# Layer 0 of a two-layer trunk: index queries earlier, query scaling from level 1 of the search, one choice of keys ahead of attention instead of two, and level 6 of the recurrence's differences on ScalarE

## What is computed

```python
h = rms_norm(x, norm_mix_g[0])
z = h @ even_w_in[0]
aq, ak, av, iq, ik, iw, bq, bf, bi, bg = split_cols(z, EVEN_SPLITS)
aq = apply_rope(rms_norm(aq), cos, sin);  ak = apply_rope(rms_norm(ak), cos, sin)
iq = apply_rope(iq, cos_i, sin_i);        ik = apply_rope(ik, cos_i, sin_i)
# dsa_attention, for each block of 128 queries: an index score of all keys,
sc = einsum('bqhd,bsd->bqhs', iqb, ik)
score = einsum('bqhs,bqh->bqs', relu(sc) * IDX_DIM ** -0.5, iwb * IDX_HEADS ** -0.5)
_, sel = top_k(where(causal, score, -inf), 256)     # the 256 keys that a query may see
# ... then softmax attention of 8 heads (2 key heads) over the keys in sel
# hgrn2: a gated recurrence of 4 heads, in chunks; bt is the running sum of log f
att = einsum('bhtd,bhsd,bhtsd->bhts', qt, kt, exp(bt[:, :, :, None] - bt[:, :, None]))   # t >= s
o = att @ vt + (qt * exp(bt)) @ state
state = exp(b_last) * state + (kt * exp(b_last - bt)).T @ vt
x = x + concat(o_a, o_b) @ even_w_out[0];  x = x + square(relu(rms_norm(x) @ w_up)) @ w_down
```

## Time and profile before

| what | value |
|---|---|
| median of 3 runs | 2616.02 us (2614.91 to 2616.26) |
| profiled execution | 2613.89 us |
| its span in the trace | 2612.2 us |
| TensorE's mean granted clock | 0.969 |
| busy: PE, DVE, ACT, POOL | 2473.1, 1617.1, 1046.7, 1295.2 us |
| chain that ended last | PE 80%, DVE 11%, issue 4%, ACT 3%, POOL 2% |

### The profile page before, as it was taken

How to read it: one execution, slowest core, us unless ns; L and a number is a source line. 1 busy time by engine, 2 the same in 40 slices (tenths; PEclk the granted TensorE clock), 3 DMA queues, 4 the chain that set the end, 5 groups by cost and what they waited for, 6 DMA issues and landing times.

```text
span 2612.2 us, 31005 instructions
## 1 busy us (share of the span) xinstructions
PE 2473.1 (95%) x11111; PEld 1967.7 (75%) x11133; DVE 1617.1 (62%) x2334; ACT 1046.7 (40%) x1759; POOL 1295.2 (50%) x682
## 2 busy tenths in 40 slices
PE   6889797899989999999999999989999999999999
PEld 5677676455887788888888887757678888888887
DVE  6578779867995545644456756675355444654483
ACT  4255786556554323322222246444453222232220
POOL 4101233768873456654567621154516546664490
PEclk8999899899999999999999999979899999999999
DMA  4211123001300112111221231121201112211121
GB/s 146 60 30 29 41 61 93 17 13 30 108 9 17 51 62 64 56 40 32 64 64 32 73 109 41 33 83 32 52 33 53 36 40 64 64 42 39 48 64 65
DMA packets 164088, 136.67 MB, mean 52 GB/s; under 512 B 22985, under 2 KB 137746, under 8 KB 163986
## 3 DMA queue, kind: packets, MB, share of 16 engines
q1 hardware_dynamic: 152978, 125.10, 15.8%
q10 hardware_dynamic: 11008, 10.23, 1.5%
HBM read 116.17 MB, written 13.63 MB: 50 GB/s over the span
## 4 chain that ended last, share of the span: by engine, by line
PE 80%; DVE 11%; issue 4%; ACT 3%; POOL 2%; DMA 0%; ACTq 0%; DVEq 0%; POOLq 0%
PE ps L2342 23%; PE ps L2344 23%; PE ps L2343 23%; PE ps L2574 1%; PE ps L2562 1%; PE ps L2754 1%; PE ps L2582 1%; PE ps L2335 1%; PE ps L2476 1%; ACT signs L1337 1%; DVE ub L2229 1%; DVE ps L1887 1%; PE ps L2573 1%; DVE shared L2226 1%; DVE acc L2173 1%
## 5 line engine op out<-in xcount | busy, mean ns | idle before, releaser
L2342 PE MATMUL ps<-h_hi,w_hi 128*128 128x512 f32 x1680 | 669.3, 398 | 9.6 <-DVE h_lo L1639 4.3
L2343 PE MATMUL ps<-h_lo,w_hi 128*128 128x512 f32 x1680 | 658.4, 392 | 0.0
L2344 PE MATMUL ps<-h_hi,w_lo 128*128 128x512 f32 x1680 | 658.1, 392 | 0.0
L781 POOL TENSOR_TENSOR w_lo<-w_raw,w_hi 128x1024 fp32r<-128x1024 f32 x73 | 194.3, 2662 | 371.8 <-ACT w_hi L1347 366.7
L2342 PEld LDWEIGHTS ps<-h_hi,w_hi 128*128 128x128 f32 x1680 | 318.5, 190 | 77.8 <-issue 8.1
L2343 PEld LDWEIGHTS ps<-h_lo,w_hi 128*128 128x128 f32 x1680 | 318.5, 190 | 67.5 <-issue 3.8
L2344 PEld LDWEIGHTS ps<-h_hi,w_lo 128*128 128x128 f32 x1680 | 318.0, 189 | 67.6
L799 POOL TENSOR_TENSOR w_lo<-w_raw,w_hi 128x1024 fp32r<-128x1024 f32 x112 | 267.9, 2408 | 168.8 <-ACT w_hi L1214 88.9
L2226 DVE TENSOR_TENSOR x_res<-ps,x_res 128x1024 f32<-128x1024 f32 x224 | 268.9, 1221 | 115.7 <-PE ps L2344 115.7
L2207 DVE TENSOR_TENSOR u_all<-ps,u_all 128x512 f32<-128x512 f32 x112 | 77.4, 691 | 388.9 <-ACT u_all L1225 388.8
L2342 PE MATMUL ps<-w_hi,uo_hi 128*128 128x512 f32 x784 | 307.9, 393 | 3.3 <-DVE shared L2226 3.3
(11 more groups left out here) (353 smaller groups left out, 4439.5 us busy)
## 6 DMA issues: line engine op xcount, KB each, us to landing
w_raw<-in_mlp_w_up SPq DMA_DIRECT2D x64, 512.0 KB, 4.0
w_raw<-in_mlp_w_down SPq DMA_DIRECT2D x64, 512.0 KB, 3.6
w_raw<-in_even_w_in SPq DMA_DIRECT2D x23, 512.0 KB, 3.8
x_res<-in_x SPq DMA_DIRECT2D x16, 512.0 KB, 8.1
w_raw<-in_odd_w_in SPq DMA_DIRECT2D x10, 512.0 KB, 3.8
scr_x<-x_res SPq DMA_DIRECT2D x8, 512.0 KB, 2.6
x_res<-scr_x SPq DMA_DIRECT2D x8, 512.0 KB, 4.3
out<-x_res SPq DMA_DIRECT2D x8, 512.0 KB, 2.6
```

The source lines that it names most:

```text
L781: g.tensor_tensor(w_lo[:, k, :], w_raw[:, n % 2, :], w_hi[:, k, :].bitcast(F32), ALU.subtract).then_inc(w_ready, 1)
L2342: t_.matmul(out_, ah, bh, start=first, stop=False)
L2343: t_.matmul(out_, ah, bl, start=False, stop=False)
L2344: return t_.matmul(out_, al, bh, start=False, stop=last)
```

## The change

Four things are changed, all in layer 0.

1. **Index queries.** `small_arguments` goes from p = 8 to 4, `small_results` and the exponential ahead of it from p = 10 to 6. The high and low parts of the index queries 2 and 3 go from p = 10 to 9, their moves from 11 to 10, and ikH of the first key half goes behind the evictions of half 11 instead of ahead of them.
2. **Scaling of queries** stands after levels 1, 2, 3, 4, 5, 7, 8, 10 instead of 4, 5, 6, 7, 9, 10, 11, 12.
3. **Choice of keys.** Block 3's is made within attention, in steps 1 to 4; those of blocks 4 to 7 move later. The signs of blocks 6 and 7 are turned back at steps 0 and 2 of attention instead of half 53.
4. **Recurrence.** For level 6 (`L_WHOLE`), where the block is the whole chunk, VectorE forms no difference. ScalarE reads bT itself, one head at a time, with the middle as bias; for the second half the negated middle `neg_mid` is the bias, which one VectorE instruction writes once into the tile mx.

```diff
+        neg_mid = mx[:].rearrange("p (h c) -> p h c", h=4)
...
-        SCALED = {4: 0, 5: 1, 6: 2, 7: 3, 9: 4, 10: 5, 11: 6, 12: 7}
+        SCALED = {1: 0, 2: 1, 3: 2, 4: 3, 5: 4, 7: 5, 8: 6, 10: 7}
...
-        CHOSEN_AT = {n: (q, part) for q, ns in ((4, (1, 2, 3, 4)), (5, (6, 8, 10, 12)), (6, (14, 16, 18, 20)),
-                                                (7, (22, 25, 28, 31))) for part, n in enumerate(ns)}
+        CHOSEN_AT = {n: (q, part) for q, ns in ((3, (1, 2, 3, 4)), (4, (6, 7, 9, 10)), (5, (12, 14, 16, 18)),
+                                                (6, (20, 22, 25, 28)), (7, (30, 33, 36, 39))) for part, n in enumerate(ns)}
...
                     q = block_begun(layer, n)
                     if q is not None:
+                        if layer == 0 and q < 2:
+                            restore_signs(6 + q)
...
-                    if p == SC_FIRST - 2:
+                    if p == 6:
                         act.wait_ge(small_arg, 1)
                         s.activation(sm[:, 0:12], sm[:, 0:12], ACT.Exp).then_inc(small_exp, 1)
+                    if p == SC_FIRST - 2:
+                        index_query_move(2)
+                        index_query_move(3)
+                    if p == SC_FIRST - 3:
                         act.wait_ge(rope_done, rope_index(0, "iq", 3, 1) + 1)
                         index_query_high(2)
                         index_query_high(3)
                     if p == SC_FIRST - 1:
                         index_key_copy(0)
-                        index_query_move(2)
-                        index_query_move(3)
-                        index_key_high(0)
...
                         rope_part(0, kind, j, hf, p)
+                    if p == SC_FIRST - 1:
+                        index_key_high(0)
...
-                    if 51 <= p < 54:
+                    if 51 <= p < 53:
                         act.wait_ge(thr_ready, 1)
                         for q in (2 * (p - 50), 2 * (p - 50) + 1):
                             restore_signs(q)
...
-                    act.wait_ge(hg["diff"], n + 1)
-                    s.activation(e[:, :, 0:B], e[:, :, 0:B], ACT.Exp, scale=-1.0).then_inc(hg["exp"], 1)
-                    s.activation(e[:, :, B:2 * B], e[:, :, B:2 * B], ACT.Exp).then_inc(hg["exp"], 1)
+                    if l == L_WHOLE:
+
+                        act.wait_ge(hg["mid"], 1)
+                        act.wait_ge(hg["att"], 8 * c + L_WHOLE - RING + 2)
+                        for h in range(4):
+                            mid = c * P + B - 1
+                            ins = s.activation(e[:, h, 0:B], bT[:, h, c * P:c * P + B], ACT.Exp, scale=-1.0,
+                                               bias=bT[:, h, mid:mid + 1])
+                        ins.then_inc(hg["exp"], 1)
+                        for h in range(4):
+                            ins = s.activation(e[:, h, B:2 * B], bT[:, h, c * P + B:(c + 1) * P], ACT.Exp,
+                                               bias=neg_mid[:, h, c:c + 1])
+                        ins.then_inc(hg["exp"], 1)
+                    else:
+                        act.wait_ge(hg["diff"], 6 * c + l + 1)
+                        s.activation(e[:, :, 0:B], e[:, :, 0:B], ACT.Exp, scale=-1.0).then_inc(hg["exp"], 1)
+                        s.activation(e[:, :, B:2 * B], e[:, :, B:2 * B], ACT.Exp).then_inc(hg["exp"], 1)
...
-                if p == SC_FIRST - 4:
+                if p == 4:
                     small_arguments()
-                if p == SC_FIRST - 2:
+                if p == 6:
                     small_results()
+                if p == SC_FIRST - 3:
                     index_query_low(2)
...
-            for q in (2, 3):
-                for part in range(4):
-                    choose_keys(q, part)
+            for part in range(4):
+                choose_keys(2, part)
...
+                if n == 2:
+                    dve.wait_ge(att["diag_ready"], 2 * T)
+                    dve.wait_ge(b_ready, 8)
+                    v.tensor_scalar(neg_mid, bT[:, :, P // 2 - 1::P], -1.0, None, ALU.mult).then_inc(hg["mid"], 1)
...
-                if c < T:
+                if c < T and l != L_WHOLE:
```

3 lines of the change are left out of this document (2 added, 1 removed).

## The result

| | before | after |
|---|---|---|
| median | 2616.14 us (2614.91 to 2616.83, 4 runs) | 2588.43 us (2586.57 to 2589.4, 4 runs) |
| profiled execution, its span | 2613.89, 2612.2 us | 2589.4, 2587.7 us |
| busy: PE, DVE, ACT, POOL | 2473.1, 1617.1, 1046.7, 1295.2 us | 2471.5, 1609.7, 1056.3, 1293.9 us |

The ratio is 0.9898, 95% interval [0.9885, 0.9912]. The same changed kernel, measured once more on another occasion, had a median of 2583.78 us (2582.46 to 2589.6, 4 runs), ratio 0.9885 [0.9868, 0.9902]. The predicted time was 2590 us, in a range of 2579 to 2602.

The account below looks back on a forecast made before the run. TensorE was taken to bound the kernel, so only its idle time in layer 0 counts. -6.3 - 10 - 4.9 - 5 = -26.2 us from 2613.89 gives 2587.7, forecast as a 2590 us median, range 2579 to 2602.

Parts of the forecast that it names:

- A: First index scores, half 12: earlier small instructions, query parts and moves start the first score near 118.05 instead of 124.37, -6.3 us.
- ikL (0.69, to 117.8): Last step before the first score: VectorE makes the first key half's low part in 0.69 us, ending at 117.8.
- the prediction's own bound for that, -3.6: First index scores: gain of only 3.6 us if POOL's next rounding (2.7 us) takes VectorE's turn.
- B: Query scaling in the search: TensorE's 13.1 us of waits go, ScalarE comes second; -10 us taken.
- The first rival: Search: TensorE waits for ScalarE's evictions, leaving 3 of B's 10 us, 2597 us; 0.27 for one of the first three.
- C: Block 3's choice moved from ahead of attention into it: logits 4.9 us sooner, -4.9 us taken.
- the second rival: Attention steps 1 to 4: VectorE's added 5 us give C back, 2595 us; 0.27 for one of the first three.
- D: Recurrence, level 6: VectorE is spared eight differences, 10.2 us as measured, of which half arrives; -5 us.
- the halving by chunks: Recurrence: TensorE is near its floor in chunks 1 to 4, waits in the other four, so half the saving arrives.
- the weighed rule: Two-input VectorE and SBUF-reading GpSimd instructions exclude each other; by it D would be worth 2.7 us, the sum -23.9.
- The third rival: Recurrence: TensorE and POOL bind every chunk, D is 0, 2595 us; 0.27 for one of the first three.
- the fourth: Recurrence: ScalarE's eight exponentials become the chain, up to 24.7 us cost, 2619.7 us; 0.06 with anything else eating the gain.

Follow-up runs that it names:

- key_low_first: Changed kernel with ikL of the first key half issued ahead of half 10's rotation on VectorE instead of behind it; 2583.68 us, ratio 0.9883.
- exp_twice: Changed kernel with ScalarE making level 6's eight exponentials a second time in each chunk; 2594.21 us, ratio 0.9916.

## Why the prediction was right, point by point

The total, 2590 us against 2588.43 and 2583.78, is right in the main for the reason it gave: idle time of TensorE in layer 0 that VectorE or ScalarE ended, and nothing from 800 us on. Against the 26.2 us forecast the medians fell by 27.7 and, the second time, 32.1 us. Its four terms are of different quality.

**A, -6.3 predicted, -4.0 measured.** Its own sign, under 2.5 us of idle time ahead of the scores, did not come: it was 4.27. The chain was right up to the last link. The step that was mis-sized: "ikL (0.69, to 117.8)". The undisturbed duration was taken although the order lets POOL's w_lo begin just then; the prediction's own bound for that, -3.6, was the nearer value. key_low_first shows it: the stall moves to whichever VectorE instruction comes just after w_lo. That w_lo would begin right there could be seen in the order: w_hi follows directly on ikH on ScalarE.

**B, -10 predicted, -9.3 without the clock's share, -6.8 in the first trace.** Right as a mechanism. TensorE's stall of 13.1 us went, and up to half 44 ScalarE's levels hold TensorE up in its place, about where the prediction had it (half 42): their chain is 9.6 us shorter against 10.5 of waits counted. The first rival (B mostly given back by evictions) also happened, but only for what the levels could not follow: of the 16.7 us won by half 39, 6.7 to 9.3 are left at half 53. The cost of the clock was named with "a few matmuls"; where it comes it is 2.1 to 2.7 us.

**C, -4.9 ahead of the logits predicted, -4.5 measured; 0 inside attention predicted, -4.9 in the first pair and -3.1 by the medians of the traces.** The first number is right; the wait for the first KS fell to 5.7 us, a little below the 6 to 8 forecast. The step that failed is that moving the choices of blocks 4 to 7 was costed at nothing, and that VectorE's 5 us more in steps 1 to 4 would be at most neutral. They cost 5.6 us, more by the medians (the second rival, "attention gives C back", which came true for block 3's choice alone), and the late steps gave 8.8 to 10.3 us, which I had not worked out at all. Most of both goes with a granted clock of 0.97 instead of 0.93, a term that the prediction's C does not have. What the earlier trace rows showed, VectorE 160 of 201 us busy in attention, was read as a risk for what is added, and not as a hint that the place of what is already there may cost something.

**D, -5 predicted, -5.5 measured** by the medians of the traces in the recurrence (-4.5 up to the end of the span), -6.0 in the first pair; by the totals the ratio is 0.9925 without it, 0.9898 and 0.9885 with it. The number holds, its working is not shown: half of the stretched 10.2 us gives 5.1, and the undisturbed 0.69 us of all eight gives 5.5 without the halving by chunks. The 2.7 us by which the weighed rule and the halving together priced it look too low, so one of the two was probably wrong, and the runs don't say which. The third rival (D nothing) is out, and so is the fourth: exp_twice puts the price of 21.6 us more on ScalarE at 3.3 to 6.3 us, while the rival needed all of it.

The rule itself is borne out at ikL: 2.83 us beside a w_lo that started 0.08 us earlier, 0.69 us without. The Trainium skill, page "SBUF — State Buffer", section "Who interferes with whom", says just this, and that the order of issue decides who waits; in key_low_first it is the rotation that started second and took 2.73 us.

**What was luck.** The first trace of before began 2.2 us late, which no step of the prediction has. Term A was too large by 2.3 us, and by the first pair of traces B was too large by 3.2 and C and D too small by 4.5 and 1.0. These errors cancel. The unforeseen gain inside attention made up for most of what A and B fell short.

## What to carry to other kernels

Give a short instruction that someone waits for its place ahead of the partner engine's long ones, and look in the order, not only in the trace, for which long one begins just then. When work is spread over a loop's steps, try the spacing of what is already there before moving more in: here the spacing was worth 9 to 10 us and the added piece cost more than it saved. And compare at marks inside the program over several traces before a difference of 1 to 4 us is given a cause.

## What the runs showed of the hardware

TensorE's granted clock after the same idle time of about 2 us is not the same in every execution. In half 13 (1.9 to 2.0 us idle) and half 14 (2.4 us) the clock over the stretches above was 1.00 and 0.89 in one execution and 0.88 and 0.77 in another of the same code, and each half took 1.4 to 1.6 us longer at the lower one. These stretches, with halves 12, 40 and 44, where quick and slow values differ by about 1 us each, add up to nearly what single runs of the changed kernel differ by, 7 us (2582.46 to 2589.6). What decides which value comes is open. With 1.0 to 1.3 us of idle time ahead of half 12 instead of 4.3, all three traces had the higher clock over halves 12 and 13.

The same VectorE instruction took 0.69 or 2.83 us by what GpSimd did: ikL took 0.69 us by itself and 2.83 us when it began 0.08 us behind a w_lo of 2.36 us.
